# Plain fp32 output products between the blocks of a state-space layer's last group, and a value projection with its features on partitions

## What is computed

```python
# sliding-window attention: the second attention
q, k, v = split(h @ w_in)              # 16 query heads, 2 key/value heads of 64
q, k = rope(rms_norm(q)), rope(rms_norm(k))
probs = softmax over a window of 128 keys, with a sink per head
o = einsum('bnkgts,bnskd->bntkgd', probs, v_band)

# state-space branch: 8 groups of 4 heads, 256 channels a group
y = ssd_chunked_scan(xh * dt, dt * a, bs, cs) + xh * d_skip
y = group_rmsnorm(y * silu(z), norm_g, 8)      # one norm per group
y_ssd = y @ w_out                              # 2048 -> 1024
```

## Time and profile before

| | |
|---|---|
| median of 3 runs | 4702.11 us (4701.28 to 4702.25) |
| the profiled execution's own time | 4701.43 us |
| its span in the profile | 4699.7 us |
| granted TensorE clock, mean | 0.975 of full speed |
| DVE busy | 2489.4 us (53%) |
| ACT busy | 1453.9 us (31%) |
| POOL busy | 304.4 us (6%) |

### The profile page before, as it was taken

One profiled execution on the slowest core, in us unless ns is written; L12 is line 12 of the kernel. 1 busy time (PEld: TensorE's weight loads), 2 busy tenths in 40 slices (PEclk: granted clock), 3 DMA queues, 4 the chain that ended last, 5 costly groups with the idle time before them and its releaser, 6 DMA issues. The chain is left out here.

```text
span 4699.7 us, 58935 instructions
## 1 busy us (share of the span) xinstructions
PE 4472.2 (95%) x22158; PEld 3752.1 (80%) x22158; DVE 2489.4 (53%) x3598; ACT 1453.9 (31%) x1578; POOL 304.4 (6%) x178
## 2 busy tenths in 40 slices
PE   8999989999999999989997999899999999999997
PEld 7888658888887778879996887677778888888886
DVE  4333444333334743346776343378888884445544
ACT  3222443223222532223443122233333333222221
POOL 0000000000000000001111000000000001333331
PEclk9999989999998999989998999899999999999998
DMA  3222112223222132222111332355555566565553
GB/s 117 98 86 84 36 36 90 98 89 99 98 87 65 28 90 98 88 66 72 59 58 36 89 91 88 104 139 138 138 134 166 173 206 206 191 197 191 190 196 107
DMA packets 514507, 519.84 MB, mean 111 GB/s; under 512 B 41173, under 2 KB 475469, under 8 KB 513374
## 3 DMA queue, kind: packets, MB, share of 16 engines
q1 hardware_dynamic: 514398, 518.41, 36.1%
HBM read 444.94 MB, written 73.40 MB: 110 GB/s over the span
## 5 line engine op out<-in xcount | busy, mean ns | idle before, releaser
L78 DVE TENSOR_TENSOR w_lo<-w_raw,w_hi 128x2048 fp32r<-128x2048 f32 (+2 forms) x326 | 676.7, 2077 | 929.6 <-ACT w_hi L72 929.5
L72 ACT CAST w_hi<-w_raw 128x2048 fp32r<-128x2048 f32 (+2 forms) x326 | 557.6, 1713 | 1285.3 <-PE psum L3075 491.6
L94 PE MATMUL psum<-h_hi,w_hi 128*128 128x512 f32 x1544 | 608.6, 394 | 14.7 <-DVE w_lo L78 11.7
L95 PE MATMUL psum<-h_lo,w_hi 128*128 128x512 f32 x1544 | 602.9, 390 | 0.0
L96 PE MATMUL psum<-h_hi,w_lo 128*128 128x512 f32 x1544 | 602.9, 390 | 0.0
L94 PE MATMUL psum<-h_hi_peer,w_hi 128*128 128x512 f32 x1104 | 437.6, 396 | 23.9 <-DVE w_lo L2922 16.1
L96 PE MATMUL psum<-h_hi_peer,w_lo 128*128 128x512 f32 x1104 | 431.2, 391 | 0.0
L95 PE MATMUL psum<-h_lo_peer,w_hi 128*128 128x512 f32 x1104 | 430.8, 390 | 0.0
L3073 PE MATMUL psum<-pr_act_hi,w_hi 128*128 128x512 f32 x1024 | 398.3, 389 | 0.0
L3074 PE MATMUL psum<-pr_act_lo,w_hi 128*128 128x512 f32 x1024 | 398.3, 389 | 0.0
L3075 PE MATMUL psum<-pr_act_hi,w_lo 128*128 128x512 f32 x1024 | 398.3, 389 | 0.0
(11 more groups left out here) (462 smaller groups left out, 7509.2 us busy)
## 6 DMA issues: line engine op xcount, KB each, us to landing
w_raw<-in_ffn_w_gate_up_dram SPq DMA_DIRECT2D x176, 512.0 KB, 4.2
w_raw<-in_peer_u_dram SPq DMA_DIRECT2D x256, 256.0 KB, 5.1
w_raw<-in_peer_v_dram SPq DMA_DIRECT2D x128, 512.0 KB, 4.2
w_raw<-in_w_in_dram SPq DMA_DIRECT2D x64, 512.0 KB, 4.4
peer_hidden<-pr_q SPq DMA_DIRECT2D x64, 512.0 KB, 3.9
peer_gates<-pr_staged SPq DMA_DIRECT2D x8, 4096.0 KB, 12.9
pr_back<-peer_hidden SPq DMA_DIRECT2D x64, 512.0 KB, 6.1
pr_gate<-peer_gates SPq DMA_DIRECT2D x64, 512.0 KB, 7.1
```

What stands on the lines that cost most here:

```text
L72: c.nc.scalar.copy(c.hi[:, slot, :cols], c.raw[:, slot, :cols]).then_inc(c.hi_ready, 1)
L78: c.nc.vector.tensor_tensor(c.lo[:, slot, :cols], c.raw[:, slot, :cols], c.hi[:, slot, :cols].bitcast(F32), ALU.subtract).then_inc(c.lo_re ...
L94: c.nc.tensor.matmul(out, w_hi, x_hi, start=(n == 0), stop=False)
L95: c.nc.tensor.matmul(out, w_hi, x_lo, start=False, stop=False)
```

## The change

Two edits.

In the second attention, v is computed like the other items, with its 128 features on partitions and all 512 tokens as the moving operand: 24 products instead of 96. VectorE evicts it into `turns` with the factor row `c.factor`, behind `evict(0)`. TensorE turns it with four transposes into bank 5, between the second and the third `sum_item`, and ScalarE copies it to `v` between `square(2)` and `root(1)`. The counts of the semaphores `turned` and `probs_taken` move by one.

In the last group of the state-space layer, TensorE multiplies chunks of `y_t` that are already there by the raw fp32 weights of the first two output tiles, as plain fp32 products (`out_plain`): 14 chunks of tile 0 and 8 chunks of tile 1, put at six places of `body(last, False)`. Ahead of the first of them it waits for both weight tiles. `ssd_out` then starts with the parts of chunks 14 and 15, adds these to both tiles and chunks 8 to 13 to tile 1 as split products (30 instead of 96), and signals slot 0 as soon as its six are issued. `Split` gets an order of its own; before the loop, TensorE waits for all of it.

```diff
--- before.py
+++ after.py
@@ -771,21 +771,23 @@
 class Split:
 
 
-    def __init__(self, c, src, h, chunks):
+    def __init__(self, c, src, h, chunks, order=None):
         self.c, self.src, self.h, self.chunks = c, src, h, chunks
+        self.order = list(range(0, chunks, 2)) if order is None else order
         self.base, self.hi_done, self.lo_done = shared(c, "split", ("hi_done", "lo_done"), chunks // 2)
 
     def wait(self, pe, k):
 
-        pe.wait_ge(self.lo_done, self.base + k // 2 + 1)
+        pe.wait_ge(self.lo_done, self.base + self.order.index(k - k % 2) + 1)
 
     def scalar(self, first, last):
-        for k in range(first, last, 2):
+        for k in self.order[first // 2:last // 2]:
             self.c.nc.scalar.copy(self.h[0][:, k:k + 2, :], self.src[:, k:k + 2, :]).then_inc(self.hi_done, 1)
 
     def vector(self, dve, first, last):
-        for k in range(first, last, 2):
-            dve.wait_ge(self.hi_done, self.base + k // 2 + 1)
+        for n in range(first // 2, last // 2):
+            k = self.order[n]
+            dve.wait_ge(self.hi_done, self.base + n + 1)
             self.c.nc.vector.tensor_tensor(self.h[1][:, k:k + 2, :], self.src[:, k:k + 2, :],
                                            self.h[0][:, k:k + 2, :].bitcast(F32), ALU.subtract
                                            ).then_inc(self.lo_done, 1)
@@ -1345,7 +1347,7 @@
                                      bias=row_of(c, "sw_sinks")[:, head:head + 1]).then_inc(weighed, 1)
 
             def take_probs(n, e):
-                act.wait_ge(turned, 2 * n + e + 1)
+                act.wait_ge(turned, 2 * n + e + 2)
                 nc.scalar.copy(probs_t[:, e].rearrange("p t b n -> p (t b n)"),
                                ps[:, 5:7, :].rearrange("p b n -> p (b n)")).then_inc(probs_taken, 1)
 
@@ -1363,6 +1365,8 @@
             square(1)
             root(0)
             square(2)
+            act.wait_ge(turned, 1)
+            nc.scalar.copy(v[:, :, :], ps[:, 5, :].rearrange("p (t n) -> p t n", t=TC)).then_inc(probs_taken, 1)
             root(1)
             root(2)
             for n in (2, 3):
@@ -1473,12 +1477,11 @@
             for t in (sin, cos):
                 step(v_.tensor_scalar(t[:, :], t[:, :], 3.1415925, -3.1415925, ALU.min, ALU.max))
             assert count[0] == ANGLES
-            dve.wait_ge(c.tile_used, 2 * u0 + 4)
-            v_.tensor_tensor(v[:, :, :], ps[:, 1, :].rearrange("p (t n) -> p t n", t=TC),
-                             c.col[:, :].unsqueeze(2).broadcast_to([P, TC, P]), ALU.mult).then_inc(v_taken, 1)
             split_lo(c, dve, *tile(1), KD * P)
             entry.take_factor(dve)
             evict(0)
+            dve.wait_ge(c.tile_used, 2 * u0 + 4)
+            v_.tensor_tensor(turns[:, :], ps[:, 1, :], c.factor[:, :], ALU.mult).then_inc(v_taken, 1)
             evict(1)
             dve.wait_ge(sined, 2)
             step(v_.tensor_scalar(cos[:, :], cos[:, :], rotary[:, 0:1], still[:, 0:1], ALU.mult, ALU.add))
@@ -1548,6 +1551,8 @@
 
             def turn_weights(n, e):
                 pe.wait_ge(norm_steps, (2 * n + e + 1) * NORM)
+                if n == 0 and e == 0:
+                    pe.wait_ge(probs_taken, 1)
                 for t in range(TC):
                     for b in range(2):
                         m = 2 * t + b
@@ -1557,7 +1562,7 @@
 
             def outputs(n, e):
                 half = slice(e * HEAD, (e + 1) * HEAD)
-                pe.wait_ge(probs_taken, 2 * n + e + 1)
+                pe.wait_ge(probs_taken, 2 * n + e + 2)
                 if e == 0 and n:
                     pe.wait_ge(o_taken, n)
                 for t in range(TC):
@@ -1577,16 +1582,18 @@
             entry.sums(pe)
             wait_tile(c, pe, u0, 1)
             w_hi, w_lo = w_tile(c, 1, KD, P)
-            for t in range(TC):
-                tok = slice(t * P, (t + 1) * P)
-                mm = products(c, ps[:, 1, tok], [
-                    ((h[0][:, k, tok], h[1][:, k, tok]), (w_hi[:, k, :], w_lo[:, k, :])) for k in range(KD)])
-            mm.then_inc(c.tile_used, 1)
+            products(c, ps[:, 1, :], [((w_hi[:, k, :], w_lo[:, k, :]), (h[0][:, k, :], h[1][:, k, :]))
+                                      for k in range(KD)]).then_inc(c.tile_used, 1)
             entry.widen(pe)
             for n in range(2):
                 project_item(n)
-            for y in range(3):
-                sum_item(y)
+            sum_item(0)
+            sum_item(1)
+            pe.wait_ge(v_taken, 1)
+            for t in range(TC):
+                mm = nc.tensor.transpose(ps[:, 5, t * P:(t + 1) * P], turns[:, t * P:(t + 1) * P], c.ident[:, :])
+            mm.then_inc(turned, 1)
+            sum_item(2)
             for y in range(3):
                 turn_item(y)
             for e in range(2):
@@ -2112,11 +2119,25 @@
                                                  c.ident[:, :])
                 mm.then_inc(y_turned, 1)
 
+            def out_plain(j, chunks):
+
+                for k in chunks:
+                    nc.tensor.matmul(ps[:, j, :], raw_tile(c, j, 2 * KD, P)[:, k, :], y_t[:, k, :], start=(k == 0),
+                                     stop=False, skip_group_check=True)
+
             def body(i, more):
                 if more:
                     channels(i + 1, 0)
+                else:
+                    for j in range(2):
+                        wait_tile(c, pe, u0 + 2 * GROUPS, j)
+                    pe.wait_ge(raw_taken, 8 * GROUPS)
+                    pe.wait_ge(y_taken, 2 * (last - 1))
+                    out_plain(0, range(0, 2))
                 if not (isinstance(i, int) and i == 0):
                     turn_y(i - 1)
+                if not more:
+                    out_plain(0, range(2, 2 * last - 2))
                 if more:
                     channels(i + 1, 1)
                     channels(i + 1, 2)
@@ -2132,18 +2153,26 @@
                                  stop=True).then_inc(advanced, 1)
                 first_half(i, 0)
                 first_half(i, 1)
+                if not more:
+                    out_plain(0, range(2 * last - 2, 2 * last))
                 second_half(i, 0)
                 first_half(i, 2)
                 second_half(i, 1)
                 if more:
                     channels(i + 1, 3)
                 first_half(i, 3)
+                if not more:
+                    out_plain(1, range(0, 1))
                 second_half(i, 2)
                 if more:
                     gates(i + 1, 0)
+                else:
+                    out_plain(1, range(1, 3))
                 second_half(i, 3)
                 if more:
                     gates(i + 1, 1)
+                else:
+                    out_plain(1, range(3, OUT_PLAIN))
 
             pe.wait_ge(meta_loaded, 16)
             for k in range(KD):
@@ -2197,14 +2226,20 @@
     return go
 
 
+OUT_PLAIN = 8
+
+
 def ssd_out(c, w, src, y, out, following):
+
 
     nc = c.nc
     u0 = c.use
     pairs = KD // 2
     with ExitStack() as ph:
         taken = sem(c, "so_taken")
-        pre = Split(c, src, y, 2 * KD)
+        late = range(2 * KD - 2, 2 * KD, 2)
+        order = [*late, *range(OUT_PLAIN, 2 * KD - 2, 2), *range(0, OUT_PLAIN, 2)]
+        pre = Split(c, src, y, 2 * KD, order)
         ps = c.psum
         block = ph.enter_context(nc.Block())
 
@@ -2246,9 +2281,18 @@
                 w_hi, w_lo = w_tile(c, j, 2 * KD, P)
                 return lambda k: ((w_hi[:, k, :], w_lo[:, k, :]), (y[0][:, k, :], y[1][:, k, :]))
 
-            for j in range(2):
+            for j, chunks in ((0, range(2 * KD - 2, 2 * KD)),
+                              (1, (*range(2 * KD - 2, 2 * KD), *range(OUT_PLAIN, 2 * KD - 2)))):
                 wait_tile(c, pe, u0, j)
-            products_as_ready(c, pe, pre, [(ps[:, j, :], pairs_of(j), c.tile_used) for j in range(2)])
+                for k in chunks:
+                    pre.wait(pe, k)
+                    (w_hi, w_lo), (y_hi, y_lo) = pairs_of(j)(k)
+                    nc.tensor.matmul(ps[:, j, :], w_hi, y_hi, start=False, stop=False, skip_group_check=True)
+                    nc.tensor.matmul(ps[:, j, :], w_hi, y_lo, start=False, stop=False, skip_group_check=True)
+                    mm = nc.tensor.matmul(ps[:, j, :], w_lo, y_hi, start=False, stop=(k == chunks[-1]),
+                                          skip_group_check=True)
+                mm.then_inc(c.tile_used, 1)
+            pre.wait(pe, order[-1])
             with pe.Fori(1, pairs) as i:
                 for j in range(2):
                     wait_tile(c, pe, u0 + i, j)
```

## The result

The changed kernel takes **4668.51 us** (median of 4 runs, 4666.78 to 4675.25) against 4701.72 for the kernel before (4 runs, 4701.28 to 4702.25): a ratio of 0.9928, with a 95% interval from 0.9917 to 0.994. The forecast was 4672.5 in 4662 to 4684. The profiled execution took 4669.01, its span 4667.2, at a mean granted clock of 0.981 (before: 4699.7 and 0.975).

The account below looks back on a forecast made before the run. TensorE, busy 4472.2 of 4699.7 us, was taken as the bound. Terms -10.9 - 1.8 - 16.9 = -29.6 on the profiled 4701.43 gave 4671.8, stated as 4672.5 us against the runs' median, range 4662 to 4684.

Parts of the forecast that it names:

- The price of a plain product: Last group, TensorE: 0.86 us at full clock, about 1.72 at half, against 0.68 for a split chunk.
- Rival 4: Plain products on raw fp32 tiles cost much more; gain gone at 2.2 us each, 4720 us at 3.0; chance 0.03.
- Part 1: Second attention, v as 24 wide products: -11.5 + 0.6 = -10.9 us, between -8 and -15.
- The tile of item 2: Second attention: its low part, made behind the sines, is late next, ready at 1487.05; a new TensorE wait of 2.6 us.
- +0.6 for ScalarE's copy: Second attention: copying v ahead of `root(1)`, for which VectorE and the scores wait, loses 0.6 us.
- Rival 1: Second attention: v is hidden anyway, its 14 us return as waits, about 3 left; 4680 us, chance 0.11.
- Part 2a: Last group with inserted plain products: +2.5 - 2.4 + 0.5 - 1.5 - 0.9 = -1.8 us, between -4 and +3.
- Rival 2: Clock stays at 0.50 all through the last group, stalls of 17.4 us eat the state-space gain; 4691 us, chance 0.10.
- Part 2b: Output stage, `take_y` to second tile: 13.5 us instead of 30.4, VectorE last; -16.9, between -15 and -18.5.
- Rival 5: Output stage: the early free slot brings nothing; a late raw tile loses 2 to 4 us, 4675; chance counted within the forecast's 0.72.
- The -18.5 bound: Output stage, best case: the slow clock behind the 3.71 us wait goes too, -18.5 us instead of -16.9.
- Rival 3: Gain given back later, as the following stage waits for transfers or VectorE; 4702 us, no change, chance 0.04.

Follow-up runs that it names:

- e10: The changed kernel once more with no edit, in a later series: 4667.36 us, ratio 0.9927 to the kernel before.
- e11: The changed kernel with one chunk of v in place of eight, 21 products left out, so v is wrong: 4672.76 us (one run).
- e8: The changed kernel with weight waits tile by tile, re-ordered output stage, 12 chunks of tile 1, item 2's high part ahead of the sines: 4668.52 us.
- e3: The kernel before with the 22 plain products in the last group, output stage unchanged, their results thrown away: 4700.65 us, ratio 0.9993.
- e6: The changed kernel with tile 2's split between the two halves of `Split` and chunks taken as they become ready: 4665.18 us, ratio 0.9918.
- e4: The kernel before with all products of output tile 0 ahead of tile 1's, no plain products: 4695.89 us, ratio 0.9985.
- e2: The changed kernel with the second attention as before, so the state-space edit alone: 4682.66 us, ratio 0.9955 to the kernel before.
- e7: The changed kernel with 14 chunks of tile 1 as plain products instead of 8: 4675.98 us, ratio 0.994 to the kernel before.
- e5: The changed kernel with each weight tile waited for only where its first product stands: 4667.37 us, ratio 0.9924 to the kernel before.

## Why the prediction was right, point by point

**The price of a plain product** was right: 0.86 at full clock (8.59 us for ten), 1.72 at half (3.45 for two). A row of all 22 (durations in ns: least, median, greatest):

```profile
L2125 PE MATMUL psum<-mix_y_t,w_raw x44: 592/592/1192, 2502.8 to 2543.4; 128*128 128x512 f32 x44
```

There are two records each, with a median of 592 as in the earlier trace rows. By the rule of four passes that the prediction weighed ("FP8 and Floating Point Precision", TensorE Precision Notes, of the Trainium skill) the ten would take 9.1; the trace has 8.6. Rival 4 (more than 2.2 us a product) is out: weights from raw tiles cost no more.

**Part 1.** The tile of item 2 was forecast to be ready 14.59 us behind v's first product and was ready after 14.5 in the changed kernel, in e10 and in e11: the term that decides was right to 0.1 us. The first `sum_item` came 12.27 earlier, where 11.5 was said; the difference is item 2 at full clock, the faster of the two values that the prediction had and not the one it took. v's own time (5.4 at full clock, 10.2 at half; measured 5.55 and 7.2) doesn't matter, since the wait takes up what it leaves. The transposes cost nothing, as said.

The prediction has v's old 19.4 us as 128-wide products at 1.2 GHz and doesn't say what each of the two costs. In the kernel before, the first narrow products of v still ran at full clock, and their steps are 0.11 us, half of a 512-wide step (0.227) for a quarter of the columns:

```profile
1472.83 0.27 PE L94 MATMUL psum<-w_hi,h_hi 128*128 128x128 f32 x1
1472.94 0.27 PE L95 MATMUL psum<-w_lo,h_hi 128*128 128x128 f32 x1
```

At half clock, at which nearly all of the 96 ran, a narrow step is 0.21 (from 1474.20 to 1474.41). So at full clock the old v would have taken some 11 us (an estimate, 96 x 0.11): each column is twice as dear in a narrow product, and the clock doubles that again. Why narrow products cost this is not shown.

The step of Part 1 that failed is the one behind the first `sum_item`: +0.6 for ScalarE's copy and nothing else. From `sum_item` to the projection the changed kernel took 1.2 us less in one execution and 3.3 less in the other (152.01 and 149.96 against 153.23). Up to the scores e10 has 11.60 against 11.26, so what the change adds there costs 0.3, not 0.6 (the changed kernel's profiled execution has 12.69, as its clock falls earlier, in the first `turn_item`). The gain lies in the last stretch of the attention, from 117 us behind `sum_item` on: 36.45 us before, 33.81 in the changed kernel, 32.85 in e10. The granted clock is higher there. Windows of 15 us at about the same place of the work, first of before:

```profile
1625.00:1640.00 15.00, 12.89 (x51) 10.20 (x50) 10.57 (x16) 5.91 (x17) 0.00 (x0) 0.66 0.00 0
1640.00:1655.00 15.00, 9.68 (x57) 8.23 (x55) 6.46 (x11) 5.32 (x16) 0.00 (x0) 0.77 0.00 0
```

Then of the changed kernel, and of e10:

```profile
1612.00:1627.00 15.00, 12.88 (x61) 9.59 (x59) 12.80 (x17) 7.56 (x21) 0.00 (x0) 0.77 0.00 1
1627.00:1642.00 15.00, 10.10 (x62) 8.54 (x62) 6.31 (x10) 7.46 (x21) 0.00 (x0) 0.89 0.00 1
...
1611.80:1626.80 15.00, 11.75 (x75) 9.12 (x75) 13.97 (x18) 9.21 (x26) 0.00 (x0) 1.00 0.00 0
1626.80:1641.80 15.00, 8.73 (x49) 7.28 (x47) 5.83 (x11) 5.11 (x15) 0.00 (x0) 0.77 0.00 1
```

The seven executions with v changed, and neither e8's nor e11's edit, have 149.9 to 152.1 from `sum_item` to the projection; the four with the old v have 153.2 to 154.8, and the last stretch at 36.4 to 36.5. But e11 has it at 36.47 too, with the whole edit of the attention in it, the same 11.60 up to the scores as e10 and only products of v left out. So neither the transposes nor the copy bring this gain. It hangs on how the clock stands when that stretch begins, and what sets that is open: that the forecast has no term for it is the step that failed, and that it came out as a gain is luck. The prediction's bound of -15 for Part 1 held it. Rival 1, v hidden anyway, was right in its mechanism as far as the changed kernel goes (e11: the last 21 products of v are worth nothing) and wrong in its size: what the tile left to gain was 12.3 us, not 3.

**Part 2a.** Up to the metadata block +2.34 (said: +2.5), with the idle time of 4.54 (4.5), the two products at half clock in 3.45 (3.4) and the ten in 8.59 (8.6). Behind it -4.93 (said: -2.4 + 0.5 - 1.5 - 0.9 = -4.3). The clock rose with the wide products and stayed up, so Rival 2 is out; PEclk is 1.00 where 0.66 and 0.53 stood. Sum -2.6 for -1.8, shown by e3 by itself.

**Part 2b.** 13.48 forecast as 13.5, ended by VectorE's `w_lo`: -16.95 for -16.9. TensorE's 30 products took 8.63 us (2550.61 to 2559.24), between the 6.8 and 12.8 of the two clocks. e6 shows that VectorE's order was the bound, and e4 and e2 how the gain divides. Rival 5 is answered too: the high part was ready at 2557.66, before VectorE came to it. The -18.5 bound named the slow clock behind the 3.71 us wait; that term did come, though a wait of 2.11 was left: the second tile's 48 products take 11.01 us instead of 12.62, of which 0.95 is left at the end of the span.

**The sum.** -12.27 - 1.22 - 2.59 - 16.95 = -33.0 in the cuts, for -29.6: the miss of 3.4 is 1.8 us in the attention's later stretch, 0.8 in item 2's clock, 0.8 in the group. Rival 3 (given back later) is out: from the projection to `gates` 851.74 against 851.90. Ahead of v, where nothing differs, the executions lie between 1472.3 and 1476.4: no ledger of a single execution is better than these 4 us, except between two instructions near each other.

## What to carry to other kernels

Price an edit by which chain is last behind it, not by the time taken off: v lost 12 us of TensorE's time and could have lost 5 more for nothing, because a tile's low part was due 14.5 us behind its start. Work that costs more per piece (0.86 against 0.68) still pays in an idle stretch, twice over where it keeps the clock up, but only until the stretch is full (e7) and only if it doesn't open another (e5). And where an engine serves two consumers, its order can be worth as much as its work (e4, e6).

## What the runs showed that was not expected

- One kernel, one code, two patterns of the clock: 149.96 and 152.01 us for the same 150 us of attention (e10 and the changed kernel), and 7.2 or 5.55 us for the same 24 products.
- Taking 21 products away made the stage 1.56 us longer (e11): the wait of 4.88 us that they left was followed by products at half clock (seven records of 0.63), while behind waits of 0.82 and 2.46 us the clock stayed up.
- The clock's fall isn't told by the idle time just ahead alone: behind 3.13 us (e5) and 3.71 us it was low, behind 2.11 and 2.46 us it was not; but in the changed kernel it fell in the middle of v, whose 24 products follow each other without a gap. In e10 it did not fall there, behind the same position row and one-column products.
